# The MLPs of a four-layer decoder in products of 512 columns: x's high and low halves side by side going up, token-major with a turn back going down, stages entered in halves of x

## The reference, cut to what matters

```
def rmsnorm(x, gain):
    y = xf * lax.rsqrt(jnp.mean(xf * xf, axis=-1, keepdims=True) + RMS_EPS)
    return y * gain

def sqrelu_mlp(h, w1, w2):          # w1 [1024, 4096], w2 [4096, 1024]
    a = jax.nn.relu(h @ w1)
    return (a * a) @ w2

for i in range(4):
    x = x + mixer_i(rmsnorm(x, norm_mix[i]))
    x = x + sqrelu_mlp(rmsnorm(x, norm_mlp[i]), mlp_w1[i], mlp_w2[i])
return rmsnorm(x, norm_final)
```

## Time and profile before

| | |
|---|---|
| median of 3 runs | 1254.59 us |
| profiled execution, its own time | 1255.52 us |
| its span | 1253.4 us |
| TensorE busy | 1206.9 us, 96% |
| VectorE busy | 803.2 us, 64% |
| ScalarE busy | 630.3 us, 50% |
| granted TensorE clock, mean | 0.988 of full speed |
| HBM traffic | 161 GB/s over the span |

### The profile page before, as it was taken

The page is one execution under the profiler, slowest core; times in us unless marked ns, Lnnn a source line. Parts: engine busy times, 40 slices in busy tenths (PEclk is TensorE's granted clock), DMA queues, the critical chain, the costliest instruction groups (busy, mean ns, idle before and its releaser), DMA issues.

```text
span 1253.4 us, 22191 instructions
## 1 busy us (share of the span) xinstructions
PE 1206.9 (96%) x9363; PEld 1170.1 (93%) x9363; DVE 803.2 (64%) x808; ACT 630.3 (50%) x707; POOL 42.7 (3%) x40
## 2 busy tenths in 40 slices
PE   6999899999999999999997999999989989999997
PEld 5999889999999999999996999999878989999997
DVE  6777767655666656656557675556877767655654
ACT  6955564444453445444435444445885575534441
POOL 2000010000010001000001100000100001000000
PEclk9999999999999999999998899999999999999999
DMA  9442344645356444545445355545433324554520
GB/s 340 153 135 101 101 135 142 225 171 191 144 204 217 142 130 152 202 171 195 171 152 200 124 191 199 192 174 193 160 109 106 121 78 147 191 201 161 200 108 34
DMA packets 84594, 202.55 MB, mean 162 GB/s; under 512 B 3253, under 2 KB 5383, under 8 KB 84272
## 3 DMA queue, kind: packets, MB, share of 16 engines
q1 hardware_dynamic: 84496, 201.58, 46.4%
q0 software_dynamic: 32, 0.02, 0.0%
HBM read 200.52 MB, written 1.06 MB: 161 GB/s over the span
## 4 chain that ended last, share of the span: by engine, by line
PE 84%; DVE 8%; ACT 4%; issue 2%; DMA 1%; SPq 0%; DVEq 0%; ACTq 0%
PE hb L559 10%; PE hb L561 10%; PE hb L560 10%; PE acc L589 9%; PE acc L591 9%; PE acc L590 9%; PE hb L511 4%; PE hb L514 4%; PE hb L513 4%; DVE wlo L1260 3%; PE acc L672 2%; PE hb L527 2%; PE hb L528 2%; PE hb L526 2%; ACT whi L929 1%
## 5 line engine op out<-in xcount | busy, mean ns | idle before, releaser
L1260 DVE TENSOR_TENSOR wlo<-raw,whi 128x2048 fp32r<-128x2048 f32 x186 | 425.1, 2317 | 197.6 <-ACT whi L929 197.5
L929 ACT ACTIVATE whi<-raw 128x2048 fp32r<-128x2048 f32 x186 | 347.0, 1903 | 144.1 <-PE acc L591 121.2
L559 PE MATMUL hb<-xh,whi 128*128 128x256 f32 x1024 | 293.0, 286 | 7.0 <-DVE xT L1656 2.9
L561 PE MATMUL hb<-xh,wlo 128*128 128x256 f32 x1024 | 291.1, 284 | 0.0
L560 PE MATMUL hb<-xl,whi 128*128 128x256 f32 x1024 | 291.1, 284 | 0.0
L589 PE MATMUL acc<-arena_r,whi 128*128 128x256 f32 x1024 | 290.4, 284 | 0.0
L591 PE MATMUL acc<-arena_r,wlo 128*128 128x256 f32 x1024 | 290.0, 283 | 0.0
L590 PE MATMUL acc<-arena_r,whi 128*128 128x256 f32 x1024 | 289.9, 283 | 0.0
L559 PEld LDWEIGHTS hb<-xh,whi 128*128 128x128 f32 x1024 | 197.8, 193 | 8.5 <-DVE xT L1656 3.3
L560 PEld LDWEIGHTS hb<-xl,whi 128*128 128x128 f32 x1024 | 197.8, 193 | 0.1
L561 PEld LDWEIGHTS hb<-xh,wlo 128*128 128x128 f32 x1024 | 197.8, 193 | 0.0
(11 more groups left out here) (217 smaller groups left out, 1635.5 us busy)
## 6 DMA issues: line engine op xcount, KB each, us to landing
raw<-in_mlp_w_dram SPq DMA_DIRECT2D x128, 1024.0 KB, 5.4
raw<-in_a_w_in_dram SPq DMA_DIRECT2D x32, 1024.0 KB, 5.4
raw<-in_b_w_qkv_dram SPq DMA_DIRECT2D x12, 1024.0 KB, 6.8
raw<-in_a_w_out_dram SPq DMA_DIRECT2D x8, 1024.0 KB, 5.1
raw<-in_b_w_out_dram SPq DMA_DIRECT2D x4, 1024.0 KB, 5.1
arena<-in_x_dram SPq DMA_DIRECT2D x1, 1024.0 KB, 5.3
arena<-in_decay_dram SPq DMA_DIRECT2D x1, 1024.0 KB, 10.8
arena<-bias_rows SPq DMA_DIRECT2D x1, 1024.0 KB, 5.9
```

The costliest lines, as they stand in the source:

```text
L559: pe.matmul(o, h, xh[:, kt, :], start=kt == 0 and q == 0, stop=False, skip_group_check=True)
L561: mm = pe.matmul(o, l, xh[:, kt, :], start=False, stop=kt == KT - 1, skip_group_check=True)
L929: act.activation(whi[:, g % 2, u, 0:n], raw[:, g % 2, u, 0:n], ACT.Copy).then_inc(hi_done, 1)
L1260: dve.tensor_tensor(wlo[:, g % 2, u, 0:n], raw[:, g % 2, u, 0:n], whi[:, g % 2, u, 0:n].bitcast(F32), ALU.subtract).then_inc(lo_done, 1)
```

## The change

- Up: `xh` and `xl` lie side by side in one tensor `xhl`. The high part of the weights is multiplied by both in one product of 512 columns (high result | low result in a bank of its own for each block of 128 hidden features), the low part by `xh` alone, 256 columns onto the high result. So an up-product fills the four banks `hb` and `misc`. ScalarE copies the low results out (`act_u`), VectorE adds the high ones to them, then does max(., 0) x rstd in one pass; ScalarE squares twice, once in float32 (`act_s`) and once rounded (`hh`), VectorE subtracts. A pair of banks is free after VectorE's sum (semaphore `summed`).
- Down: the hidden part is stationary and w2 moves, 512 columns, so that a bank `acc[2c + t]` has 128 tokens x 512 features. At the end ScalarE copies the banks to `y_tok` (`y_copy`), TensorE transposes them (`back_transposes`, 8 transposes for each half c of the features) into `out_banks`, and VectorE adds from there.
- Entry: the first up-product and an early group take tiles 0 to 3 of x for all their banks, then tiles 4 to 7. `take_x` makes the low parts of x in fours. The second half of the transposes stands in the next layer's first group after its first quarter; the sum over squares comes after the third quarter and the column after the fourth (before: second and third). The sum's bank is `acc[3]` for the MLP.
- In layers 0, 1 and 3 the split of w1's first group is spread over `take_x`; in layer 2 the second half of w1's split comes behind the pool mixer's low parts. Layers 1 and 2 write their outputs to all four `out_banks` and do not wait for a bank.

```diff
-        xh = sb("xh", [P, KT, SEQ], F32R)
-        xl = sb("xl", [P, KT, SEQ], F32R)
+        xhl = sb("xhl", [P, KT, 2, SEQ], F32R)
+        xh, xl = xhl[:, :, 0, :], xhl[:, :, 1, :]
...
+        up_pairs = [hb_pair, misc_pair]
+        def ms_bank(n):
+            if n == 2 * DEPTH:
+                return hb[0]
+            return acc[3] if n % 2 else misc[0]
...
                 def step():
                     at[0] += 1
-                    if at[0] == 2:
+                    if at[0] == 1 and n:
+                        back_transposes(n // 2 - 1, 1)
+                    if at[0] == 3:
                         ones_mm(n)
-                    if at[0] == 3:
+                    if at[0] == 4:
                         token_column(n)
...
+                        h, l = (w_k(t, g, kt, f * P, (f + 1) * P) for t in (whi, wlo))
+                        pe.matmul(o[:, :], h, xhl[:, kt, :, :], start=kt == 0, stop=False, skip_group_check=True)
+                        mm = pe.matmul(o[:, 0:SEQ], l, xh[:, kt, :], start=False, stop=kt == KT - 1,
+                                       skip_group_check=True)
...
+                if r_at is None:
+                    for half in range(2):
+                        for f in range(4):
+                            if half == 0:
+                                pe.wait_ge(x_ready, 4 * (2 * layer + 1) + 1 + f)
+                            mm = tile(f, 4 * half, 4 * half + 4)
+                            if half and f % 2:
+                                mm.then_inc(bank_ready, 1)
+                    return
                 for i in range(2):
+                    pe.wait_ge(summed, r_at + (i - 1))
...
             def mlp_down(layer, g, par, lo_at, hl_at, first=False, last=False):
+                for c in range(2):
+                    for t in range(TT):
+                        o = acc[2 * c + t][:, :]
+                        for kt in range(4):
...
+                            ys, yl = (y[:, par, kt, t * P:(t + 1) * P] for y in (hh, hl))
+                            pe.matmul(o, ys, h, start=first and kt == 0, stop=False, skip_group_check=True)
+                            pe.matmul(o, ys, l, start=False, stop=False, skip_group_check=True)
+                            mm = pe.matmul(o, yl, h, start=False, stop=last and kt == 3, skip_group_check=True)
+                        if last:
+                            mm.then_inc(acc_ready, 1)
+                            if c == 1 and t == 0:
+                                back_transposes(layer, 0)
...
+            def back_transposes(layer, c):
+                pe.wait_ge(y_sb, 4 * layer + 2 * c + 2)
+                for k in (2 * c, 2 * c + 1):
+                    for f in (2 * k, 2 * k + 1):
+                        for t in range(TT):
+                            at = (f % 2 * TT + t) * P
+                            mm = pe.transpose(out_banks[k][:, at:at + P], y_tok[:, 2 * c + t, f % 4 * P:(f % 4 + 1) * P],
+                                              ident[:, :])
+                    mm.then_inc(back_mm, 1)
...
-                        act.activation(act_r[:, i, :], hb[i][:, :], ACT.Relu).then_inc(relu_done, 1)
+                        act.activation(act_u[:, i, :].rearrange("p (a b) -> p a b", a=2), up_pairs[i][:, :, SEQ:2 * SEQ],
+                                       ACT.Copy).then_inc(low_sb, 1)
                         if first and i == 0:
                             rms(n + 1)
+                        act.wait_ge(scaled_done, r_at + (i + 1))
...
+                        act.activation(act_s[:, i, :], act_u[:, i, :], ACT.Square)
...
                         act.activation(hh[:, par, 2 * i:2 * i + 2, :],
-                                       act_s[:, i, :].rearrange("p (a b) -> p a b", a=2), ACT.Copy)\
+                                       act_u[:, i, :].rearrange("p (a b) -> p a b", a=2), ACT.Square)\
                             .then_inc(hh_done, 1)
...
+                def y_copy(i):
+                    act.wait_ge(acc_ready, 4 * layer + i + 1)
...
+                    act.activation(y_tok[:, i, :], acc[i][:, :], ACT.Copy).then_inc(y_sb, 1)
+                for i in range(3):
+                    y_copy(i)
+                take_x(n + 2, {1: lambda: y_copy(3)})
...
                 for k in range(4):
                     update(k)
-                    if n < 2 * DEPTH and k:
-                        lo(2 * k - 2)
-                        lo(2 * k - 1)
+                    if n < 2 * DEPTH and k % 2:
+                        for f in range(2 * k - 2, 2 * k + 2):
+                            lo(f)
...
-                take_x(n + 1, mixed, {} if layer % 3 == 2 else {1: lambda: split(g)})
+                take_x(n + 1, mixed, {} if layer % 3 == 2 else {1: lambda: split_unit(g, 0), 2: lambda: split_unit(g, 1)})
...
+                        dve.wait_ge(low_sb, r_at + (i + 1))
+                        dve.tensor_tensor(z, up_pairs[i][:, :, 0:SEQ], z, ALU.add)\
+                            .then_inc(summed, 1)
+                        if first and i == 0:
+                            dve.wait_ge(rstd_ready, n + 2)
+                        dve.wait_ge(summed, r_at + (i + 1))
+                        dve.scalar_tensor_tensor(out=z, in0=z, scalar=0.0,
+                                                 in1=rstd[:, :].rearrange("p (a b) -> p a b", a=1)
+                                                 .to_broadcast([P, 2, SEQ]),
+                                                 op0=ALU.max, op1=ALU.mult).then_inc(scaled_done, 1)
```

More of the change, by code:

```diff
@@ L452, in ones_mm @@
                 for i in range(2):
-                    mm = pe.matmul(misc[0][:, 0:SEQ], ones[:, :], hn[:, i, :], start=i == 0, stop=i == 1)
+                    mm = pe.matmul(ms_bank(n)[:, 0:SEQ], ones[:, :], hn[:, i, :], start=i == 0, stop=i == 1)
                 mm.then_inc(ms_mm, 1)
@@ L564, in mlp_up @@
-                for i in range(2):
-                    if r_at is not None:
-                        pe.wait_ge(relu_done, r_at + (i - 1))
-                    else:
-                        pe.wait_ge(x_ready, 4 * (2 * layer + 1) + 3 + i)
-                    k0 = 0
-                    if r_at is None and i == 0:
-                        k0 = 6
-                        for q in range(2):
-                            tiles(i, q, 0, k0)
+                        h, l = (w_k(t, g, kt, f * P, (f + 1) * P) for t in (whi, wlo))
@@ new lines, in mlp_down @@
+                if not last:
+                    mm.then_inc(down_done, 1)
+            def back_transposes(layer, c):
[7 more added lines that the diff above has]
+                    mm.then_inc(back_mm, 1)
@@ L628, in acc_read @@
                     def acc_read(k):
-                        pe.wait_ge(x_ready, 4 * n + k + 1)
-                    group("W", g0, 0, acc_read, need, norm_steps(n), acc[0:2])
+                        if layer:
+                            pe.wait_ge(y_sb, 4 * (layer - 1) + k + 1)
+                        else:
+                            pe.wait_ge(x_ready, 4 * n + k + 1)
+                    group("W", g0, 0, acc_read, need, norm_steps(n), acc[0:2], early=True)
                     group("W", g0 + 1, 2, lambda k: None, need, banks=acc[2:4])
@@ L902, in _ @@
                     pe.wait_ge(rstd_ready, n)
-                mm = pe.matmul(misc[0][:, 0:SEQ], ones[:, :], hn[:, f, :], start=f == 0, stop=f == KT - 1)
+                mm = pe.matmul(hb[0][:, 0:SEQ], ones[:, :], hn[:, f, :], start=f == 0, stop=f == KT - 1)
             mm.then_inc(ms_mm, 1)
@@ L1204, in _ @@
                 g = first_group[f"mlp{layer}"]
-                take_x(n + 1, {} if layer % 3 == 2 else {1: lambda: split(g)})
+                take_x(n + 1, {} if layer % 3 == 2 else {1: lambda: split_unit(g, 0), 5: lambda: split_unit(g, 1)})
                 g, b = first_group[f"mlp{layer}"], first_bank[f"mlp{layer}"]
@@ L1324, in _ @@
                 j = layer // 3
-                split(g0 + 1)
-                if layer % 3 != 1:
+                split_unit(g0 + 1, 0)
+                if layer % 3 == 2:
+                    column(n)
+                else:
+                    split_unit(g0 + 1, 1)
+                if layer % 3 == 0:
                     column(n)
@@ L1654, in mixed @@
                     else:
-                        ob = hb[k % 2] if layer == 1 else out_banks[k]
+                        ob = out_banks[k]
                         ch.did(dve.tensor_tensor(xT[:, pair, :], ob[:, :].rearrange("p (a b) -> p a b", a=2),
```

133 lines of the change are left out of this document (63 added, 70 removed).

## The result

The changed kernel takes 1245.93 us (median of four runs, 1245.39 to 1247.74) against 1254.12 for the kernel before (four runs): ratio 0.9939, 95% interval 0.9926 to 0.9952, so 8.2 us faster, give or take 1.6. Forecast were 1238 and 16.6 us. The profiled execution shows 1245.68 with a span of 1243.4, and a mean granted clock of 0.988 as before.

The account below looks back on a forecast made before the run. TensorE, busy 96%, was taken as the bound. Pace -34.1, transposes +7.0, first chunks and entry +3.7, exits +4.6 and end +1.9 gave -16.9 us, about 1238; 8 in 10 for 1229 to 1247.

Parts of the forecast that it names:

- the pace, -34.1: MLP products on TensorE: fewer, longer products save 13.6 us in the up-products and 20.5 in the down-products.
- Rival 3: Up-product: 256 columns behind 512 in one bank cost what they save, only the down-product gains; 1251 us, chance 0.06.
- Transposes, +7.0: Turning the down-product back: 64 new transposes of 0.109 us each on TensorE's path, 7.0 us.
- Seams, +10.2 in all: Added waits at MLP entries, first chunks, exits and program end, beside pace and transposes: +3.7, +4.6 and +1.9 us.
- Entry of layers 0 and 3: First two chunks: waits of 1.8 us for the last x pair and 2.0 for the first sum; +1.4 per layer.
- Layer 0's exit, +0.6: End of layer 0's MLP: 0.3 us for late low parts of x and 0.3 for the squares' sum.
- Layer 1's exit, +1.25: Layer 1's MLP end to the third up-product: first transposes wait 2.0 us, partly regained; +1.25 without transposes, slow clock kept.
- Layer 2's exit, +2.75: Into layer 3's mixer: column 15.3 us after the first product, gate chain absorbs nothing; +4.5, of which 1.75 are transposes.
- End, +1.9: Program end: last x pair 4.6 us after the product instead of 0.95; +3.65 less 1.75 for transposes.
- Rival 1: Seams cost only their transposes: -25.2 us in all, 1229 to 1230 us, chance 0.25.
- Rival 2: ScalarE and VectorE bound the loop: each of 28 pairs waits 0.5 us, +14, 1252 us; chance 0.08.
- Rival 4: Slower: a 512-column product costs two of 256, nothing is saved; +17.2 us, 1272 us, chance 0.04.

Follow-up runs that it names:

- experiments under 2: Up-product of the changed kernel varied: all products 512 columns wide, 1338.05 us; 512s first in each bank, 1242.40; two of a kind, then two of the other, 1241.96.
- the doubling: Changed kernel with each of the 64 transposes back issued twice into the same place: 1251.57 us, ratio 0.9983 to the kernel before.
- the early bias row: Changed kernel with VectorE's copy of layer 1's bias row moved ahead of its two low parts of weights: 1243.10 us, ratio 0.9918 to the kernel before.
- the late copy: Changed kernel with ScalarE's fourth copy of the down-product's banks behind its other x work, except at the program's end: 1245.10 us, ratio 0.9939 to the kernel before.

## Why the prediction missed

- **The step that failed: the pace, -34.1.** "512 columns cost 0.227 and 256 cost 0.120, also in mixed company" came from one change of width, at a change of bank, in the earlier trace rows. The changed kernel's pair costs 0.353, not 0.347: some 6 ns of the 13.3 saved are lost, 0.2 an up-product, and the down-product behind it takes 10.95 for 10.88. By the rows the term is 32 x 0.81 = 25.9, 26.0 unrounded, so 8.1 short. Span against span the miss is 6.9 (16.9 forecast, 10.0 measured): these 8.1, less 1.2 by which the seams came cheaper. Median against median it is 8.4; the rest is where the two profiled executions lie among their runs. That the alternation costs the pace is shown by the experiments under 2; with two of a kind side by side the loop is 22.03, within 0.06 of the forecast. In time that gives back 4.1 (good to 2.5), where 32 x 0.20 = 6.4 was to be had: about half of the miss is shown by a run, the other half by the starts alone. Rival 3 had named this mechanism with its full loss (0.06); half of it happened.
- **Transposes, +7.0:** right within the noise. The earlier trace rows give 0.80 for eight from start to start, not the 0.87 that was read from them, which would be 6.4 in all; eight added ones cost 0.87 in the doubling (1.66 against 0.79), and the doubling as a whole 5.5 (2 to either side).
- **Seams, +10.2 in all:** +9.0 measured, right in the sum, in the parts only by luck. Entry of layers 0 and 3 as worked out: 1.78 for the x pair (forecast 1.8), 1.54 for the first sum in layer 3 (2.0). In layer 0 of the profiled execution the first sum is no wait, but the clock fell to 0.68 in its place, which the forecast did not have; other executions of the same instructions show the wait, 1.5. The working had two slips: 33.06 + 4.7 against 38.1 is 0.3 gained, which beside the 1.5 of the pace makes +1.2 for each of the two layers, not +1.4; and in layer 1 the wait of 1.45 did not come (0.0 measured for +0.9).
- **Layer 0's exit, +0.6: too small by 2.7.** The column of layer 1 was looked at, the bias row copied by VectorE just ahead of it was not. "TensorE waits for nothing in that mixer until its end" was only true as long as ScalarE waited 2.7 us for that row's DMA, as in the kernel before, and not 6.8. Shown by the early bias row (2.6 less).
- **Layer 1's exit, +1.25: too dear by 4.5 together with layer 2's entry.** The wait ahead of the first transposes, worked out at 2.0, was 0.7; and the slow clock of the earlier trace rows, left as it was within +-3, went away: 694 to 700 at 1.00. It was left "since those waits stay", and they did not: TensorE's wait in the pool mixer for VectorE fell from 4.1 to 2.5, the longest one for an x pair at layer 2's entry from 2.3 to 1.1. Why they shrank is open. The wait of 1.40 for the first sum (at 700.87) took part of the gain back.
- **Layer 2's exit, +2.75, layer 3's entry +1.4:** 3.9 for 4.15. But the place was wrong: the column came 14.3 behind the mixer's first product (10.7 before, forecast 15.3), and yet TensorE still waits 4.80 at the decay; 2.11 stand earlier, at 896.82, for VectorE's low weights queued behind the gates.
- **End, +1.9:** +1.8, though the parts listed for it add up to 4.8 and not to 4.6.
- The waiting of ScalarE for the last quarter of the down-product is there (1.54 us ahead of the fourth copy at 365.73) and costs nothing that the late copy could show.
- Rival 1 (seams cost only transposes): refuted, they cost 15.2 with 7.0 for the transposes. Rival 2 (the loop bound by VectorE): TensorE has no wait from 242 to 362, 746 to 862 and 1105 to 1224, within the loops of layers 0, 2 and 3. Rival 4: refuted by the down-product's 17.9.

What stays open: what in TensorE makes a lone 256-column product cost some 6 ns more. The last section narrows it down.

## What to carry to other kernels

A pace must be read from a stretch of the same pattern; one boundary between two patterns said nothing about alternating them here, and where short and long products alternate, two of each side by side can be worth a try: here they took 4.1 us off. A stretch of low clock in one trace should be looked for in the traces of other executions before a term is given to it. Price what a change adds by running it without what it saves: here 15.2 us of added work had stood hidden behind a net of -8. When a producer becomes late, follow everything on its queue up to the next DMA, not only the item whose consumer is known.

## What the hardware showed

The alternating pattern has two paces. In the changed kernel most stretches of eight pairs (half overlapping) run at 0.351 to 0.355 a pair, but some 8% of them (15 of about 180) at 0.346 to 0.348, with the same instructions. All of these lie in the first three up-products of a layer, none in the five later ones. The three that I followed begin behind an irregularity: the 0.53 wait at 221.87, the sums' products of 128x256 at 494.11, and at 724.58 a single pair that took 0.39. Layer 1's second up-product:

```profile
499.48 0.40 PE L576 MATMUL hb<-xhl,whi 128*128 128x512 f32 x1
499.71 0.28 PE L577 MATMUL hb<-xhl,wlo 128*128 128x256 f32 x1
499.83 0.39 PE L576 MATMUL hb<-xhl,whi 128*128 128x512 f32 x1
500.06 0.27 PE L577 MATMUL hb<-xhl,wlo 128*128 128x256 f32 x1
500.17 0.40 PE L576 MATMUL hb<-xhl,whi 128*128 128x512 f32 x1
```

0.23 and 0.115 in place of 0.24 and 0.11. So the extra is not a fixed price of the order, but something like a phase that a disturbance can set; that is an inference, and no run sets it on purpose.

At the lower clock level neither extra shows. The changed kernel behind its wait at 187.57, and the window there (granted clock 0.50, the 1.2 GHz level):

```profile
189.27 0.63 PE L576 MATMUL hb<-xhl,whi 128*128 128x512 f32 x1
189.69 0.41 PE L577 MATMUL hb<-xhl,wlo 128*128 128x256 f32 x1
189.91 0.63 PE L576 MATMUL hb<-xhl,whi 128*128 128x512 f32 x1
```

```profile
189.30:191.80 2.50, 2.50 (x9) 2.11 (x9) 0.56 (x1) 2.50 (x3) 2.24 (x2) 0.50 0.81 331
```

A pair takes 0.64 us, which is 768 columns at 1.2 GHz and nothing more; at 2.4 GHz it is 0.347 or 0.353 where the columns alone would be 0.320. The 13 ns a product on which this change lives show only at the high clock. The Trainium skill ("TensorE: Matmul & The Clock Gate", section "Wait — 56ns, not 53.3ns?") says the same of its fixed part, columns alone at the low level and an addition only at 2.4 GHz; the trace agrees in that and not in the size, 13 ns for 2.5.
